# A hybrid decoder trunk on one core: the recurrence's decay by Exp, the heads' mean squares as columns, their root and split at other steps

## The chip, the cores and the metric

One core of a Trainium2 (trn2) chip runs the whole kernel. The metric is the time of one execution in microseconds; the median of the runs of the kernel before is compared with that of the kernel after. The engines are named as in the profile: PE (TensorE, matmuls; its weight loads are PEld), DVE (VectorE), ACT (ScalarE), POOL (GpSimd) and SP (SyncE, which issues the loads of the weights).

## The reference, cut to what matters

Two layers over 256 tokens of width 1024. Each layer is a token mixer, a channel mixer (a dense SwiGLU in layer 0, top 2 of 8 experts in layer 1) and a small gated embedding, each with norms around it. The change touches two places of the token mixer, the gated linear recurrence and the norm over each attention head:

```
r = sigmoid(blockdiag(u, w_a) + b_a);  i_gate = sigmoid(blockdiag(u, w_x) + b_x)
log_a = -8.0 * r * softplus(-lam)
a     = exp(log_a)
beta  = sqrt(-expm1(2.0 * log_a))
h[t]  = a[t] * h[t-1] + beta[t] * i_gate[t] * u[t]
...
o = (prob[:, 0] - lam * prob[:, 1]) @ v              # per head, 256 tokens x 128
o = o * rsqrt(mean(o * o, axis=-1) + 1e-6) * g_sub * (1.0 - lambda_init)
```

## The kernel before, in words

Every weight matrix comes in pieces ("chunks") of 128x2048 values of float32. A product of float32 accuracy is made of three products of a faster type: the chunk is split into a high part `whi` (ACT, line 630) and a low part `wlo` (DVE, line 1093), each in two halves of 1024 columns, and the activations into high and low parts in the same way (`HH`, `HL`; for the heads' outputs `YBH`, `YBL`, which lie in the same place). There are three slots for split chunks, so ACT splits chunk c+3 in step c, when PE has let go of each half of chunk c, and DVE follows it.

`mixer(layer)` is a list of steps c = 0 to 35, one chunk of weights each, written out by hand on every engine: each engine runs a loop over c and does, in the order of its code, what its `if` lines give to that step. The engines meet through semaphores alone. Each engine works strictly in order, so whatever stands behind a waiting instruction waits too.

- PE: in each step one chunk (48 products, `chunk8`, line 1743), then, by step: `gate_products` (2 to 5), `swap` for the rotary embedding (5 to 12), `scores` of head c-14 (line 1918, steps 14 to 21), `turn` (transposes of the weights of head c-16, line 1931, steps 16 to 23), `values` of head c-17, `head_square` of head c-18 (line 1951, steps 18 to 25). `inverse_row` (line 1866) transposes a column that is broadcast over 128 columns. Chunks 28 to 31 are the projection of the recurrence, 32 to 35 that of attention; chunk 32 is the first that needs `YBH` and `YBL`. Then `merge_out` (the output projection) and `embed` follow. In them `turn_x` (line 1854, four transposes of a half of X) waits for the sum of the residual. Later in layer 1, `logits` (line 2013) multiplies 128x128 weights by the 8 columns of the router.
- ACT: in each step first `hi` (the split, line 630, two halves), then copies of what PE made; `gate_functions` in steps 2 to 5 (sigmoids, and T2 = tanh(4 * r * softplus)), in step 6 the root of T2 (line 784), in step 7 T2 + 1 (786), in steps 12 and 16 the decay 2/(1 + T2) - 1 from the reciprocal (791); the exponentials of head c-14 (798, 803); Gelu in step 20 (775); Tanh of the merge gates in steps 21 to 28 (810); copies of the turned weights WT (817), of the head's output (824) and its square (825); the mean square of head c-18 copied (830); in step 28 the root of all reciprocal mean squares (836); in steps 29 and 30 the high part of the heads' outputs (840). After the mixer `square_z` (641) and `root_z` (664) make the norm of the merged output, and DVE adds it to X (line 1153).
- DVE: in each step first `lo` (line 1093), then by step: convolution (0 to 3), `rotate` (5 to 12), `recurrence_input` of tile c-8 (reciprocal line 1191, products 1192 and 1194, steps 8 to 15), `scan` in steps 13 and 17 (1200), gates scaled by the row norm (1158), `mask_max` of head c-14 (1224, 1227, 1230), `difference` of head c-15 (1235 to 1243), the reciprocal of a head's mean square in steps 19 to 26 (1334), `normalise_heads` in steps 28 and 29 (1250), `split_heads` in steps 30 and 31 (1256).
- POOL loads, once `split_heads` is through (`s_yb`), a row of gains for the norm behind the mixer. SP only issues the loads of the chunks.

The tanh form of the recurrence: with T2 = tanh(z), z = -log_a / 2, the decay is a = (1 - T2)/(1 + T2) = 2/(1 + T2) - 1 and beta = 2 sqrt(T2)/(1 + T2). The mean square of a head is a sum over the 128 partitions; a product with a matrix of ones (`ONES` as weights) gives it on every partition at once, as 128x256 values, equal in all rows.

## Time and profile before

| | before |
|---|---|
| median of 3 runs | 1862.76 us (1862.08 to 1863.0) |
| the profiled execution | 1862.89 us |
| its span, first to last instruction | 1861.2 us |
| mean granted clock of PE | 0.995 |
| PE busy | 1808.3 us, 97% of the span |
| DVE busy | 1541.8 us, 83% |
| ACT busy | 1307.3 us, 70% |
| POOL busy | 80.6 us, 4% |
| PE's share of the chain that ended last | 82% (DVE 11%, ACT 6%, issue 2%) |

The time is that of an execution, the span lies inside it: 1.7 us of the profiled execution lie around its span. Busy shares are means over stages with different limits; the two mixers (about 24 to 290 us and 570 to 835 us of the span) are where the change acts. A line of the timeline gives start, duration, engine, source line, operation, the tiles out<-in, and in brackets how long the engine had stood idle before it and what ended that; a line of the chain gives start, duration and what ran. "x4" at the end joins four instructions. Consecutive instructions of one engine overlap by about 0.1 us in the timeline, so starts are the better measure of a step.

### The profile page before, as it was taken

Reading aid. Unit: us, or ns where it says so; the run is one execution under the profiler, and the core shown is the slowest. Engines: PE = TensorE matmul, PEld = TensorE weight load, DVE = VectorE, ACT = ScalarE, POOL = GpSimd, SP = SyncE. Lnnn points to the kernel's source line nnn. Section 1 sums busy time; section 2 is a strip of 40 time slices with the busy share of each in tenths; the row PEclk is TensorE's granted clock in tenths of the full one; section 3 lists DMA queues with packets and bytes.
Section 4 is the critical chain, followed back from the end, with each engine's and each line's share of the span. In section 5 each row is a group of like instructions: output and inputs, shape, how many; then the busy total and the mean of one; then the engine's idle time right before and its main releaser. Section 6 shows DMA issues by size and latency. Waiting matters only on the chain.

```text
span 1861.2 us, 29663 instructions
## 1 busy us (share of the span) xinstructions
PE 1808.3 (97%) x10489; PEld 1573.7 (85%) x10489; DVE 1541.8 (83%) x1973; ACT 1307.3 (70%) x1730; POOL 80.6 (4%) x73
## 2 busy tenths in 40 slices
PE   6999999999999999999999999999999999999997
PEld 6998999999879988987888888888888888888785
DVE  7898877666468898768998989989899888998996
ACT  6656646444467557547878888788888887888776
POOL 1000000000010000002001000010000000000300
PEclk9999999999999999999999999999999999999999
DMA  9543456555554443557999999999999999999991
GB/s 304 161 159 130 165 172 201 183 181 198 197 173 144 160 159 114 182 194 222 390 381 385 378 372 386 368 380 380 372 387 365 382 386 366 385 372 378 391 365 54
DMA packets 274002, 512.82 MB, mean 276 GB/s; under 512 B 9731, under 2 KB 113029, under 8 KB 273925
## 3 DMA queue, kind: packets, MB, share of 16 engines
q1 hardware_dynamic: 268400, 493.81, 74.6%
q0 software_dynamic: 5200, 17.86, 2.8%
q8 instruction: 49, 0.80, 0.2%
q14 instruction: 29, 0.23, 0.0%
q10 hardware_dynamic: 324, 0.12, 0.0%
HBM read 503.87 MB, written 7.88 MB: 275 GB/s over the span
## 4 chain that ended last, share of the span: by engine, by line
PE 82%; DVE 11%; ACT 6%; issue 2%; DMA 0%; SPq 0%; DVEq 0%; ACTq 0%
PE bank L1743 77%; DVE wlo L1093 4%; ACT whi L630 2%; PE bank L2198 1%; DVE T L1191 1%; PE bank L1898 1%; ACT SC L803 1%; ACT SQJ L641 1%; DVE SC L1227 1%; DVE RIN L1200 0%; ACT HH L688 0%; PE bank L2208 0%; ACT SC L798 0%; PE bank L1854 0%; ACT L731 0%
## 5 line engine op out<-in xcount | busy, mean ns | idle before, releaser
L630 ACT ACTIVATE whi<-raw 128x1024 fp32r<-128x1024 f32 x880 | 920.4, 1059 | 330.7 <-PE bank L1743 322.4
L1093 DVE TENSOR_TENSOR wlo<-raw,whi 128x1024 fp32r<-128x1024 f32 x880 | 1030.2, 1222 | 127.1 <-ACT whi L630 123.7
L1743 PE MATMUL bank<-HH,whi 128*128 128x256 f32 x1296 | 372.6, 287 | 3.0 <-DVE HL L1256 3.0
L1743 PE MATMUL bank<-HL,whi 128*128 128x256 f32 x1296 | 362.4, 280 | 0.0
L1743 PE MATMUL bank<-HH,wlo 128*128 128x256 f32 x1296 | 362.3, 280 | 0.0
L1743 PE MATMUL bank<-whi,XGH 128*128 128x512 f32 x896 | 358.4, 400 | 1.4 <-DVE wlo L1093 1.0
L1743 PE MATMUL bank<-whi,XGL 128*128 128x512 f32 x896 | 352.2, 393 | 0.0
L1743 PE MATMUL bank<-wlo,XGH 128*128 128x512 f32 x896 | 348.9, 389 | 0.0
L1743 PEld LDWEIGHTS bank<-HH,whi 128*128 128x128 f32 x1296 | 244.1, 188 | 7.5 <-issue 6.9
L1743 PEld LDWEIGHTS bank<-HL,whi 128*128 128x128 f32 x1296 | 244.4, 189 | 3.5 <-issue 2.9
L1743 PEld LDWEIGHTS bank<-HH,wlo 128*128 128x128 f32 x1296 | 246.3, 190 | 0.0
L1743 PEld LDWEIGHTS bank<-whi,XGL 128*128 128x128 f32 x896 | 168.6, 188 | 39.6
L1743 PEld LDWEIGHTS bank<-wlo,XGH 128*128 128x128 f32 x896 | 168.8, 188 | 35.5
L1743 PEld LDWEIGHTS bank<-whi,XGH 128*128 128x128 f32 x896 | 169.0, 189 | 35.1 <-DVE wlo L1093 2.3
L1743 PE MATMUL bank<-whi,ATH 128*128 128x512 f32 x448 | 178.6, 399 | 0.0
L1743 PE MATMUL bank<-whi,ATL 128*128 128x512 f32 x448 | 175.7, 392 | 0.0
L1743 PE MATMUL bank<-wlo,ATH 128*128 128x512 f32 x448 | 174.0, 388 | 0.0
L1743 PEld LDWEIGHTS bank<-whi,ATL 128*128 128x128 f32 x448 | 84.1, 188 | 19.7
L1743 PEld LDWEIGHTS bank<-wlo,ATH 128*128 128x128 f32 x448 | 84.2, 188 | 17.8
L1743 PEld LDWEIGHTS bank<-whi,ATH 128*128 128x128 f32 x448 | 84.3, 188 | 16.0
L1442 DVE TENSOR_TENSOR wlo<-raw,whi 128x1024 fp32r<-128x1024 f32 x56 | 68.3, 1224 | 35.4 <-ACT whi L905 32.9
L905 ACT ACTIVATE whi<-raw 128x1024 fp32r<-128x1024 f32 x56 | 58.9, 1057 | 47.7 <-PE bank L1743 47.7
(348 smaller groups left out, 2123.4 us busy)
## 6 DMA issues: line engine op xcount, KB each, us to landing
raw<-in_moe_w_gate_dram SPq DMA_DIRECT2D x112, 1024.0 KB, 7.3
raw<-in_moe_w_up_dram SPq DMA_DIRECT2D x112, 1024.0 KB, 7.9
raw<-in_moe_w_down_dram SPq DMA_DIRECT2D x112, 1024.0 KB, 6.5
raw<-in_w_in_dram SPq DMA_DIRECT2D x56, 1024.0 KB, 5.1
raw<-in_ffn_w_gate_dram SPq DMA_DIRECT2D x14, 1024.0 KB, 5.0
raw<-in_ffn_w_up_dram SPq DMA_DIRECT2D x14, 1024.0 KB, 5.0
raw<-in_ffn_w_down_dram SPq DMA_DIRECT2D x14, 1024.0 KB, 4.9
raw<-in_w_proj_a_dram SPq DMA_DIRECT2D x8, 1024.0 KB, 5.2
```

Of the source, the lines that this page charges most:

```text
L630: nc.scalar.activation(whi[b % SPL][:, r], raw[b % RAW][:, r], ACT.Copy).then_inc(s_hi, 1)
L641: nc.scalar.activation(SQJ[:, :], src, ACT.Square, accum_out=sums).then_inc(s, 1)
L803: ins = nc.scalar.activation(r, r, ACT.Exp, bias=AMX[:, q, 2 + m:3 + m], scale=HD ** -0.5, accum_out=ASUM[:, q, 2 + m:3 + m])
L905: nc.scalar.activation(whi[nb % SPL][:, r], raw[nb % RAW][:, r], ACT.Copy).then_inc(s_hi, 1)
L1093: v.tensor_tensor(wlo[b % SPL][:, r], raw[b % RAW][:, r], whi[b % SPL][:, r].bitcast(F32), ALU.subtract).then_inc(s_lo, 1)
L1191: link(v.reciprocal(T2[:, i, :], T2[:, i, :]))
L1227: ins = v.tensor_tensor_reduce(SC[:, q, SEQ * (m + 1):SEQ * (m + 2)], B[4 + m][:, P:P + SEQ], MASK[:, :], 1.0, -3e38, ALU.add, ALU.max, AM ...
L1442: v.tensor_tensor(wlo[nb % SPL][:, r], raw[nb % RAW][:, r], whi[nb % SPL][:, r].bitcast(F32), ALU.subtract).then_inc(s_lo, 1)
L1743: ins = mm(dst, a, b, start=start and n == 0, stop=stop and n == 2, skip_group_check=True)
L1898: ins = mm(bank[:, SEQ * kind:SEQ * kind + SEQ], BD[:, kind, t, :], U[:, t, :], start=True, stop=True)
L2198: ins = nc.tensor.transpose(B[6][:, P * i:P * i + P], MA[:, f % 2, P * i:P * i + P], IDENT[:, :])
```

## The change

**Recurrence.** Tanh now goes into a tile of its own, `TH` (the place of K, whose keys are not made yet), and T2 keeps the gate r. In steps 7 and 8 ACT makes the decay from it directly, T2 = Exp(-8 * softplus * r), four tiles of 128x256 in each (`decays`); the factor is a new column set `SPNEG`, one product more among the constants. Since 2/(1 + tanh z) = 1 + a, beta is sqrt(TH) * (1 + a), one instruction of DVE. The eight reciprocals of T2 on DVE, T2 + 1 on ACT and the two copies of steps 12 and 16 are gone, and DVE waits for the decays at tiles 0 and 4.

**Heads' mean squares.** `head_square` now takes the squares as weights, block by block of 128 tokens, and multiplies them by one column of ones: two columns of sums for each head, tokens on the partitions, 128x16 for all heads. One Sqrt of ACT in step 25 and one reciprocal of DVE in step 25 cover all heads. In step 26 PE spreads them over the partitions again with 16 transposes of broadcast columns into banks 4 to 7 (`head_rows`). DVE multiplies the heads' outputs by these banks in steps 26 and 27 (four instructions of 128x512 in place of two of 128x1024), ACT and DVE split them in steps 27, 28 and 28, 29. The eight copies of ACT (line 830), the eight reciprocals of DVE (line 1334) and the two roots of ACT (line 836) are gone.

```diff
@@ -145,7 +145,9 @@
         SINR = at("SINR", o_sga + 7 * KB, [P, SEQ])
         top = o_sga + 8 * KB
         assert top <= end, (top, end)
-        OALL, MSALL = Q, K
+        OALL, TH = Q, K
+        SPNEG = SM[:, 72:88]
+        HSD, HRS = SM[:, 0:16], SM[:, 16:32]
         YBH, YBL = HH, HL
 
         FH = at("FH", a0 + 16 * KB, [P, FT, SEQ], F32R)
@@ -264,7 +266,6 @@
         s_ga = sem("s_ga")
         s_sq = sem("s_sq")
         s_iu = sem("s_iu")
-        s_den = sem("s_den")
         s_bl = sem("s_bl")
         s_al = sem("s_al")
         s_rt = sem("s_rt")
@@ -287,7 +288,7 @@
         s_oc = sem("s_oc")
         s_om = sem("s_om")
         s_or = sem("s_or")
-        s_oe = sem("s_oe")
+        s_hr = sem("s_hr")
         s_os = sem("s_os")
         s_yf = sem("s_yf")
         s_ybh = sem("s_ybh")
@@ -746,8 +747,15 @@
                     nc.scalar.activation(IG[:, t, :], bank[:, SEQ:], ACT.Sigmoid, bias=V2[:, 96 + col:97 + col])
                     if layer == 0 and t == 0:
                         act.wait_ge(s_c2, 1)
-                    ins = nc.scalar.activation(T2[:, t, :], T2[:, t, :], ACT.Tanh, scale=SPLAM[:, col:col + 1])
-                    ins.then_inc(s_ga, 1)
+                    nc.scalar.activation(TH[:, t, :], T2[:, t, :], ACT.Tanh,
+                                         scale=SPLAM[:, col:col + 1]).then_inc(s_ga, 1)
+
+            def decays(layer, g):
+
+                for t in range(4 * g, 4 * g + 4):
+                    col = layer * KT + t
+                    ins = nc.scalar.activation(T2[:, t, :], T2[:, t, :], ACT.Exp, scale=SPNEG[:, col:col + 1])
+                ins.then_inc(s_al, 1)
 
             def mixer(layer):
                 b = BASE[layer]
@@ -781,14 +789,9 @@
                     if c == 6:
                         act.wait_ge(s_ga, KT * (layer + 1))
                         act.wait_ge(s_iu, layer + 1)
-                        nc.scalar.activation(SQ[:, :, :], T2[:, :, :], ACT.Sqrt).then_inc(s_sq, 1)
-                    if c == 7:
-                        nc.scalar.activation(T2[:, :, :], T2[:, :, :], ACT.Copy, bias=1.0).then_inc(s_den, 1)
-                    if c in (12, 16):
-                        g = (c - 12) // 4
-                        act.wait_ge(s_bl, KT * layer + 4 * g + 4)
-                        r = T2[:, 4 * g:4 * g + 4, :]
-                        nc.scalar.activation(r, r, ACT.Copy, bias=-1.0, scale=2.0).then_inc(s_al, 1)
+                        nc.scalar.activation(SQ[:, :, :], TH[:, :, :], ACT.Sqrt).then_inc(s_sq, 1)
+                    if c in (7, 8):
+                        decays(layer, c - 7)
                     h = c - 14
                     if 0 <= h < HEADS:
                         n = HEADS * layer + h
@@ -823,19 +826,12 @@
                             act.wait_ge(s_om, n - 1)
                         nc.scalar.activation(OALL[:, h, :], B[7][:, 0:SEQ], ACT.Copy)
                         nc.scalar.activation(OSQ[:, h % 2, :], B[7][:, 0:SEQ], ACT.Square).then_inc(s_oc, 1)
-                    h = c - 18
-                    if 0 <= h < HEADS:
-                        n = HEADS * layer + h
-                        act.wait_ge(s_om, n + 1)
-                        nc.scalar.activation(MSALL[:, h, :], B[3][:, 0:SEQ], ACT.Copy, bias=EPS,
-                                             scale=1.0 / P).then_inc(s_oe, 1)
-                    if c == 28:
-                        act.wait_ge(s_or, HEADS * (layer + 1))
-                        for g in range(2):
-                            r = MSALL[:, 4 * g:4 * g + 4, :]
-                            nc.scalar.activation(r, r, ACT.Sqrt).then_inc(s_os, 1)
-                    if c in (29, 30):
-                        g = c - 29
+                    if c == 25:
+                        act.wait_ge(s_om, HEADS * (layer + 1))
+                        nc.scalar.activation(HSD[:, :], B[3][:, 0:2 * HEADS], ACT.Sqrt, bias=EPSC[:, 0:1],
+                                             scale=1.0 / P).then_inc(s_os, 1)
+                    if c in (27, 28):
+                        g = c - 27
                         act.wait_ge(s_yf, 2 * layer + g + 1)
                         nc.scalar.activation(YBH[:, 4 * g:4 * g + 4, :], OALL[:, 4 * g:4 * g + 4, :],
                                              ACT.Copy).then_inc(s_ybh, 1)
@@ -1185,12 +1181,12 @@
             def recurrence_input(layer, i):
 
                 if i == 0:
-                    dve.wait_ge(s_den, layer + 1)
                     dve.wait_ge(s_sq, layer + 1)
                     dve.wait_ge(s_iu, layer + 1)
-                link(v.reciprocal(T2[:, i, :], T2[:, i, :]))
-                link(v.scalar_tensor_tensor(out=SQ[:, i, :], in0=SQ[:, i, :], scalar=2.0, in1=T2[:, i, :],
-                                            op0=ALU.mult, op1=ALU.mult))
+                if i % 4 == 0:
+                    dve.wait_ge(s_al, 2 * layer + i // 4 + 1)
+                link(v.scalar_tensor_tensor(out=SQ[:, i, :], in0=T2[:, i, :], scalar=1.0, in1=SQ[:, i, :],
+                                            op0=ALU.add, op1=ALU.mult))
                 v.tensor_tensor(IG[:, i, :], IG[:, i, :], SQ[:, i, :], ALU.mult).then_inc(s_bl, 1)
 
             def scan(layer, g):
@@ -1245,10 +1241,12 @@
                                        op1=ALU.add).then_inc(s_df, 1)
 
             def normalise_heads(layer, g):
-                ms, o = (t[:, 4 * g:4 * g + 4, :] for t in (MSALL, OALL))
-                dve.wait_ge(s_os, 2 * layer + g + 1)
-                v.scalar_tensor_tensor(out=o, in0=o, scalar=GSUB[:, layer:layer + 1], in1=ms, op0=ALU.mult,
-                                       op1=ALU.mult).then_inc(s_yf, 1)
+                dve.wait_ge(s_hr, 2 * layer + g + 1)
+                for i in (4 * g, 4 * g + 2):
+                    o = OALL[:, i:i + 2, :]
+                    ins = v.scalar_tensor_tensor(out=o, in0=o, scalar=GSUB[:, layer:layer + 1], in1=bank2(4 + i // 2),
+                                                 op0=ALU.mult, op1=ALU.mult)
+                ins.then_inc(s_yf, 1)
 
             def split_heads(layer, g):
                 dve.wait_ge(s_ybh, 2 * layer + g + 1)
@@ -1273,6 +1271,7 @@
                     link(v.scalar_tensor_tensor(out=poly, in0=poly, scalar=1.0 / n, in1=s2, op0=ALU.add, op1=ALU.mult))
                 link(v.scalar_tensor_tensor(out=poly, in0=poly, scalar=1.0, in1=s1, op0=ALU.add, op1=ALU.mult))
                 link(v.scalar_tensor_tensor(out=poly, in0=poly, scalar=2.0, in1=SM[:, 32:48], op0=ALU.mult, op1=ALU.add))
+                v.tensor_scalar(SPNEG, poly, -8.0, None, ALU.mult)
                 v.tensor_scalar(SPLAM[:, :], poly, 4.0, None, ALU.mult).then_inc(s_c2, 1)
 
             def mixer(layer):
@@ -1328,14 +1327,13 @@
                             dve.wait_ge(s_tg, 8 * layer + 8)
                         v.scalar_tensor_tensor(out=pair(SGA, i), in0=pair(SGA, i), scalar=1.0, in1=bank2(c % 3),
                                                op0=ALU.add, op1=ALU.mult).then_inc(s_evd, 1)
-                    if 19 <= c < 27:
-                        h = c - 19
-                        dve.wait_ge(s_oe, HEADS * layer + h + 1)
-                        v.reciprocal(MSALL[:, h, :], MSALL[:, h, :]).then_inc(s_or, 1)
+                    if c == 25:
+                        dve.wait_ge(s_os, layer + 1)
+                        v.reciprocal(HRS[:, :], HSD[:, :]).then_inc(s_or, 1)
+                    if c in (26, 27):
+                        normalise_heads(layer, c - 26)
                     if c in (28, 29):
-                        normalise_heads(layer, c - 28)
-                    if c in (30, 31):
-                        split_heads(layer, c - 30)
+                        split_heads(layer, c - 28)
                     if 32 <= c < 36:
                         i = c - 32
                         if c == 35:
@@ -1946,9 +1944,17 @@
             def head_square(layer, h):
                 n = HEADS * layer + h
                 pe.wait_ge(s_oc, n + 1)
-                if h:
-                    pe.wait_ge(s_oe, n)
-                mm(B[3][:, 0:SEQ], ONES[:, :], OSQ[:, h % 2, :], start=True, stop=True).then_inc(s_om, 1)
+                for b in range(BLK):
+                    ins = mm(B[3][:, 2 * h + b:2 * h + b + 1], OSQ[:, h % 2, P * b:P * b + P], ONES[:, 0:1],
+                             start=True, stop=True, skip_group_check=True)
+                ins.then_inc(s_om, 1)
+
+            def head_rows(layer, g):
+                pe.wait_ge(s_or, layer + 1)
+                for i in range(8 * g, 8 * g + 8):
+                    ins = nc.tensor.transpose(B[4 + i // 4][:, P * (i % 4):P * (i % 4) + P],
+                                              HRS[:, i:i + 1].to_broadcast([P, P]), IDENT[:, :])
+                ins.then_inc(s_hr, 1)
 
             def mixer(layer):
                 b = BASE[layer]
@@ -1990,6 +1996,9 @@
                         values(layer, c - 17)
                     if 18 <= c < 26:
                         head_square(layer, c - 18)
+                    if c == 26:
+                        head_rows(layer, 0)
+                        head_rows(layer, 1)
 
             def merge_out(layer):
 
```

## Rows read from the trace of the kernel before

**Rows 1.** Windows (steps 15 to 22, 23 to 32): us, busy of PE, PEld, DVE, ACT, POOL, clock, DMA
```profile
127.70:187.36 59.66, 54.54 (x439) 49.85 (x439) 51.49 (x138) 40.29 (x103) 0.00 (x0) 1.00 0.43 141
187.36:246.66 59.30, 57.77 (x483) 57.03 (x483) 48.56 (x49) 36.51 (x49) 0.00 (x0) 1.00 0.49 162
```

**Rows 2.** Waits, layer 0's mixer: who <- for whom, us in total, times, longest
```profile
PE bank L1931 <- ACT WT L817: 3.9, 3, 1.4
...
PE bank L1743 <- DVE HL L1256: 1.5, 1, 1.5
```

**Rows 3.** Timeline of PE: scores of step 15, transposes of step 22
```profile
127.68 0.49 PE L1918 MATMUL bank<-K,Q 64*128 64x128 f32 x4 [0.85 <-DVE AMX L1230]
...
187.36 0.52 PE L1931 MATMUL bank<-IDENT,SC 128*128 128x128 f32 x3 [1.34 <-ACT WT L817]
```

**Rows 4.** Timeline of DVE: splits of steps 14 to 18 and 21, first maximum of step 14
```profile
123.95 2.36 DVE L1093 TENSOR_TENSOR wlo<-raw,whi 128x1024 fp32r<-128x1024 f32 x2
126.23 0.29 DVE L1224 CUSTOM_DVE_ANT_0 SC<-bank,MASK 128x128 f32<-128x128 f32 x1
...
130.51 2.36 DVE L1093 TENSOR_TENSOR wlo<-raw,whi 128x1024 fp32r<-128x1024 f32 x2 [0.31 <-ACT whi L630]
...
138.26 2.35 DVE L1093 TENSOR_TENSOR wlo<-raw,whi 128x1024 fp32r<-128x1024 f32 x2
...
145.77 2.36 DVE L1093 TENSOR_TENSOR wlo<-raw,whi 128x1024 fp32r<-128x1024 f32 x2 [1.68 <-ACT whi L630]
...
154.00 2.36 DVE L1093 TENSOR_TENSOR wlo<-raw,whi 128x1024 fp32r<-128x1024 f32 x2
...
180.15 2.36 DVE L1093 TENSOR_TENSOR wlo<-raw,whi 128x1024 fp32r<-128x1024 f32 x2 [1.97 <-ACT whi L630]
```

**Rows 5.** Timeline of ACT: step 14 and the start of 15; step 20
```profile
120.16 1.06 ACT L630 ACTIVATE whi<-raw 128x1024 fp32r<-128x1024 f32 x1 [1.70 <-PE bank L1743]
...
127.66 0.40 ACT L798 ACTIVATE SC<-SC,AMX 128x128 f32<-128x128 f32 x1 [4.42 <-DVE AMX L1230]
...
129.43 1.04 ACT L630 ACTIVATE whi<-raw 128x1024 fp32r<-128x1024 f32 x1
...
169.58 2.01 ACT L630 ACTIVATE whi<-raw 128x1024 fp32r<-128x1024 f32 x2
171.60 1.28 ACT L775 ACT_TABLE_LOAD   x1
172.90 1.92 ACT L775 ACTIVATE GEL<-GEL 128x2048 f32<-128x2048 f32 x1
```

**Rows 6.** Single lines of the source, whole span: duration in ns, min/median/max
```profile
L1191 DVE RECIPROCAL T<-T x16: 1743/1746/1749, 86.9 to 680.9; 128x256 f32<-128x256 f32 x16
L1866 PE MATMUL bank<-IDENT,STAT x6: 270/270/271, 30.4 to 576.0; 128*128 128x128 f32 x6
```

**Rows 7.** The chain of waits: start us, us, what
```profile
161.09 0.28 ACT K L830
...
189.22 5.66 PE bank L1743 x48
...
208.49 0.43 PE bank L1951 x2
...
286.29 0.44 PE bank L1854 x4
...
837.88 1.69 PE bank L2013 x16
```

**Rows 8.** Timelines of ACT and DVE behind layer 0's mixer: the root, the residual's sum
```profile
284.31 0.29 ACT L664 ACTIVATE STAT<-STAT 128x1 f32<-128x1 f32 x1
...
285.05 1.41 DVE L1153 SCALAR_TENSOR_TENSOR X<-ZG,STAT,X 128x512 f32<-128x512 f32 x2
```

**Rows 9.** Windows in layer 1: step 17, and the router's products
```profile
688.00:692.00 4.00, 2.57 (x16) 2.01 (x16) 2.29 (x6) 3.94 (x11) 0.00 (x0) 0.79 0.60 209
...
831.00:848.00 17.00, 15.85 (x95) 13.52 (x93) 11.45 (x35) 14.45 (x38) 4.58 (x8) 1.00 0.64 168
```

## The prediction, made before the result was known

> **What bounds the kernel now.** I read the windows first, then the waits, then the timelines of PE, VectorE (DVE) and ScalarE (ACT) side by side. Both mixers run the same list of steps, so I work out layer 0 and count it twice. In steps 23 to 32 PE is busy 57.77 of 59.30 us, with 10.7 us idle on DVE and 22.8 on ACT; in steps 15 to 22 PE is busy 54.54 of 59.66 us [rows 1], and 0.85 us more it stood at the edge of that window [rows 3]: 6.0 us. The list of waits puts 3.9 of them down to ACT's copy of WT, and beside them names 1.5 us for the low half of the head outputs, at step 32 [rows 2]. 6.0 and 1.5 us a mixer are what PE can win, small gaps inside a step aside.
>
> Where the 6.0 us come from takes two engines. PE is through chunk 14 at 120.16, when it lets go of the buffer that ACT waits for [rows 5]; DVE masks that step's scores only at 126.23, and neither this row nor the one at 123.95 prints a wait [rows 4]: DVE itself is 6 us late. Each of its steps from 8 on holds a reciprocal of T2 of 1.75 us [rows 6]. From there a loop closes: DVE splits (lo) and takes the maxima, ACT exponentiates, copies what PE made and splits the next chunk (hi), and only then DVE can split. DVE's splits of steps 15 to 18 start at 130.51, 138.26, 145.77 and 154.00, that of step 21 at 180.15 [rows 4]: turns of 7.75, 7.51, 8.23 and three together 26.15 us. At 138.26 no wait is printed: DVE was late, its reciprocal counts. At 145.77 and 180.15 it waits 1.7 and 2.0 us for ACT: a shorter DVE gains nothing there, only a shorter ACT. At 154.00 DVE is late by its scan, which stays.
>
> **The change part by part.** *Reciprocals of T2 out, Exp in.* DVE loses 16 reciprocals of 1.75 us over both mixers [rows 6]. In steps 8 to 13 PE never waits, so those six of a mixer's eight pay only through the lag they leave. Without them DVE keeps pace, and step 14 starts from ACT's second split at 120.16. A half split of ACT leads to DVE's by 1.08 us (129.43 to 130.51), DVE's half takes 1.14 (half of 123.95 to 126.23), and from the maxima to ACT's exponentials it is 1.43 (126.23 to 127.66) [rows 4, 5]: they start at 123.81 instead of 127.66. From there to DVE's next split is 2.85 us as before (127.66 to 130.51): 126.66 instead of 130.51, **3.85 us earlier**. In the next turn ACT's second split waits for PE's chunk, done at 126.83 (127.68 less the wait of 0.85 [rows 3]); 1.08 + 1.14 + 1.43 + 2.85 = 6.50 later, at 133.33, comes the next split. This turn takes 6.67 instead of 7.75, **1.08 us less**. The turn of 7.51 is ACT's and stays; that of 8.23 stays for the scan.
>
> The new work on ACT is eight Exp of 128x256 a mixer in steps 7 and 8. Two of 128x128 and two of 128x256 took 1.77 us (127.66 to 129.43 [rows 5]), so four of 128x256 take 1.8 to 3.5; a 2048-wide copy in step 7 and two 1024-wide ones in steps 12 and 16 go. The load of Exp's table moves from before step 14's exponential to step 7. PE runs on chunks split three steps ahead and never waits there, so this costs nothing; if that cover were gone, up to 3 us. DVE's new waits for the decays, at steps 8 and 12, stand ahead of its first use, lo and the next rotation queue behind them, and PE's swap behind these; the Exp ended a step before: nothing. The one product more (128x16, once) delays ACT's first Tanh by less than a reciprocal's 1.75 us, behind PE's products: nothing.
>
> *Mean squares as columns.* ACT's copy of each head's mean square, 0.28 us, is in the loop in steps 18 to 20 [rows 7]: three turns, **0.8 us**. The eight reciprocals of K lie beside ACT's part of the loop or where DVE is idle: nothing. PE's two records of 256 columns took 0.43 us a head; now each of two blocks has 128x128 weights and one column. The nearest row is the router's product with 8 columns, 16 records in 1.69 us [rows 7]: four records a head are 0.42 us, **no difference**. Bounds: 0.2 us less a head (two records) to 0.7 more (four times the 0.27 of a lone record [rows 6]).
>
> *Sixteen transposes at step 26* are new, and PE is the bound there: four take 0.44 us on the path [rows 7], so **1.8 us are lost**. The other end is 0.27 us each, the duration of one transpose of a broadcast column [rows 6]: 4.3 us. I take the pipelined value, since four such take less than two durations. Their input is early: after chunk 25 come half a split (1.08), a Tanh no longer than a half split, a load (1.28) and two tiny operations of 0.3, some 4.1 us at most, while PE needs 5.66 for chunk 26.
>
> *Root and split earlier.* DVE normalises at steps 26 and 27, ACT splits at 27 and 28, DVE at 28 and 29; PE reads at 32, so the stall of **1.5 us** goes. Next late would be the weight split for chunk 32, done in step 29, in time. DVE's waits at 25 and 26 (under 1 us each; lo is ahead of them in its queue, the next lo behind) fall where it is idle 10.7 us: nothing. POOL's load of the gain row waits for the split and is issued earlier.
>
> *Table loads.* Sqrt at step 25 stands between the Tanh of 25 and 26, and the norm's root comes after the mixer: loads at 25, 26 and the root instead of one at 28. Each takes 1.28 us, the next activation starts 20 ns behind [rows 5]. Those of 25 and 26 fall where ACT has 2 us idle a step. The third does not: the root ran at 284.31 without a wait, DVE's add began at 285.05 and had its first half at 285.76 (half of 1.41), PE's transpose of it began at 286.29 [rows 7, 8]. 0.5 us of slack against 1.3: **0.8 us lost**; bounds 0 and 2.1.
>
> The Trainium skill ("ScalarE: Activation LUTs", What ACT_TABLE_LOAD costs) speaks against this part: it puts a switch of tables at about 1283 ns for the load and 1380 ns of drain, 2.66 us, by which the sum would be 1.4 us a mixer worse. The trace agrees on the load and shows no drain around it [rows 5].
>
> **Sum.** 3.85 + 1.08 + 0.8 + 1.5 - 1.8 - 0.8 = 4.6 us a mixer, 9.2 us for two. From the profiled execution's 1862.89 us: 1853.7. It stands 0.1 us over the median of the runs, so I give **1853.6 us**. About 0.2%, 3.7 us, is what a measurement of this kernel can tell from no change.
>
> **Rivals.** *(1) The lag was not the reciprocals'.* If something else holds step 14's maxima back, the first 3.85 us stay: 0.8 us a mixer left, 1861.2 us, no measurable change. For it: most turns are ACT's. Against: DVE prints no wait at 123.95 and 126.23. Chance 0.10.
> *(2) Transposes in single file.* 4.3 us instead of 1.8: 2.5 us a mixer more, 1858.6. Against it the 0.44 us for four. 0.10.
> *(3) A switch of tables holds ACT for twice the load's 1.28 us.* Then 2.1 us instead of 0.8 are lost at the root, 1856.2. Against it the 20 ns behind the load. 0.07. This is the page's figure as a mechanism.
> *(4) PE's waits go altogether and the load at the root is covered.* 6.0 + 1.5 - 1.8 = 5.7 us a mixer, 1851.4. 0.09.
> *(5) Slower: the clock falls behind step 26.* In layer 1 the granted clock was 0.79 of full in 688 to 692 us, where PE was busy 2.57 of 4.00 us [rows 9]. If transposes and one-column products made it fall to the lower of its levels (1.2 GHz), each chunk of 5.66 us takes 11.3. The gain of 4.6 us a mixer is gone after 4.6 us' worth of products at that level, and from 6.5 us' worth on the kernel is measurably slower; two chunks cost 11.3 us a mixer, 1876. Against it: the 32 router products and 16 transposes in 831 to 848 us, all at 1.00 [rows 9]. 0.04.
>
> **How the numbers follow.** The forecast has 0.60, its own range being 1851 to 1857 (table load 0 to 2.1, turns 0.3 us each). Faster by over 0.2% is below 1859.0: 0.60 + 0.10 + 0.07 + 0.09 = 0.86. Within: rival 1, 0.10. Slower: rival 5, 0.04. The range 1850.5 to 1859.0 takes in rivals 2 to 4 and leaves out 0.14 and a little.
>
> **What would show it.** Right: step 14's scores are masked at about 122.4 us; DVE's turns read 6.7, 7.5, 8.2 and 25.3 for three; PE's transposes of step 22 start at 181.6 instead of 187.36; no wait of PE at step 32; sixteen transposes in 1.8 us; a load ahead of the root and behind it a wait of PE for X of 0.8 us; DVE busy 56 us less. Wrong: PE waiting for the maxima at step 15 as before or for the 16 reciprocals at step 26, a clock under 0.95 in steps 26 to 30, or waits of PE for weights in steps 8 to 13 because Exp came in the way of hi.

## The result and the profile after

The changed kernel takes 1847.2 us (median of 5 executions, 1845.92 to 1853.16) against 1862.81 of the kernel before (5 executions): ratio 0.9925, 95% interval 0.9914 to 0.9935. Faster, as forecast, but by 15.6 us and not by 9.2, and below the range. The five times lie in two groups: 1845.92, 1846.68 and 1847.2, and then 1852.61 and 1853.16. The profiled execution took 1845.92 us, of which 1844.3 are its span. From its page, the span and the busy time of each engine:

```profile
span 1844.3 us, 29748 instructions
PE 1801.3 (98%) x10553; PEld 1568.6 (85%) x10553; DVE 1490.6 (81%) x1948; ACT 1302.6 (71%) x1726; POOL 80.7 (4%) x73
```

DVE is busy 51.2 us less (forecast 56), 1541.8 to 1490.6. The windows of layer 0's mixer, steps 15 to 22 and then 23 to 32 [rows 1]:

```profile
126.55:181.60 55.05, 53.21 (x448) 49.43 (x447) 44.15 (x132) 35.85 (x90) 0.00 (x0) 1.00 0.41 135
181.60:240.40 58.80, 58.79 (x503) 58.43 (x504) 39.12 (x44) 33.98 (x43) 0.58 (x1) 1.00 0.50 170
```

In the first stretch PE stands still for 1.84 us where it stood for 5.12. In the second it stands for none, sixteen transposes included, and the clock is 1.00. DVE's splits of steps 14 to 18, with the first maximum of step 14 [rows 4]:

```profile
119.78 2.47 DVE L1089 TENSOR_TENSOR wlo<-raw,whi 128x1024 fp32r<-128x1024 f32 x2
122.16 0.28 DVE L1220 CUSTOM_DVE_ANT_0 SC<-bank,MASK 128x128 f32<-128x128 f32 x1
...
126.44 2.51 DVE L1089 TENSOR_TENSOR wlo<-raw,whi 128x1024 fp32r<-128x1024 f32 x2 [2.10 <-ACT whi L631]
...
133.15 2.52 DVE L1089 TENSOR_TENSOR wlo<-raw,whi 128x1024 fp32r<-128x1024 f32 x2 [0.50 <-ACT whi L631]
...
140.83 2.36 DVE L1089 TENSOR_TENSOR wlo<-raw,whi 128x1024 fp32r<-128x1024 f32 x2 [1.68 <-ACT whi L631]
...
149.06 2.36 DVE L1089 TENSOR_TENSOR wlo<-raw,whi 128x1024 fp32r<-128x1024 f32 x2
```

DVE now waits for ACT in every turn but that of the scan: the lag is gone, and the turns are 6.71, 7.68 and 8.23 us. PE's timeline: the scores of step 15 and the transposes of step 22 [rows 3], one group of head squares, the sixteen transposes, and the first transposes of X behind the mixer:

```profile
126.53 0.49 PE L1916 MATMUL bank<-K,Q 64*128 64x128 f32 x4
...
181.60 0.52 PE L1929 MATMUL bank<-IDENT,SC 128*128 128x128 f32 x3 [1.26 <-ACT WT L820]
...
202.20 0.50 PE L1948 MATMUL bank<-ONES,OSQ 128*128 128x1 f32 x4
...
208.30 1.91 PE L1955 MATMUL bank<-IDENT,SM 128*128 128x128 f32 x16
...
279.24 0.40 PE L1741 MATMUL bank<-whi,YAL 128*128 128x512 f32 x1
280.27 0.66 PE L1852 MATMUL bank<-IDENT,X 128*128 128x128 f32 x4 [0.63 <-DVE X L1149]
```

ACT's timeline behind the mixer has the table load ahead of the root [rows 8]:

```profile
277.64 1.28 ACT L665 ACT_TABLE_LOAD   x1
278.94 0.29 ACT L665 ACTIVATE STAT<-STAT 128x1 f32<-128x1 f32 x1
```

**Where the rest came from.** From the scores of step 14 to the transposes of step 22, the profiled executions differ by 5.53 us in layer 0 (67.31 to 61.78); up to the transposes of X behind mixer 0, by 5.9 (286.13 to 280.27). Mixer 1 gives 5.05 (254.95 to 249.90, from the transposes ahead of it to those of X). Before, the granted clock dips between the layers (0.54 in 557 to 559 us); in the change's profile it stays at 1.00 there, which takes 1.3 us out. Behind mixer 1 it dips in both, at another moment of the work, which adds 1.2. The 5.6 us that are left came between the two mixers, in the dense layer, which the change does not touch. That stretch begins with two transposes of a broadcast column inside its second chunk and reaches the down projection's first product, which reads FH, after some 1,300 products of 128x256. The kernel before:

```profile
304.45 0.38 PE L1866 MATMUL bank<-IDENT,STAT 128*128 128x128 f32 x2
...
454.49 0.40 PE L1743 MATMUL bank<-whi,FH 128*128 128x512 f32 x1
```

and the kernel after:

```profile
298.63 0.38 PE L1864 MATMUL bank<-IDENT,STAT 128*128 128x128 f32 x2
...
443.04 0.39 PE L1741 MATMUL bank<-whi,FH 128*128 128x512 f32 x1
```

150.04 us became 144.41, with the same instructions. Two windows of 20 us inside the stretch (us, PE busy, clock, DMA share, GB/s), before:

```profile
320.00:340.00 20.00, 20.00 (x172) 1.00 0.60 195
400.00:420.00 20.00, 20.00 (x173) 1.00 0.54 173
```

and after:

```profile
320.00:340.00 20.00, 20.00 (x179) 1.00 0.56 186
400.00:420.00 20.00, 20.00 (x179) 1.00 0.54 178
```

PE is busy all the time in both, at full clock in both, with a like share of DMA (0.54 to 0.60), and 172 or 173 products fall into 20 us in the one and 179 in the other, those that reach over an edge counted in. By the starts of single products, one comes every 117.8 ns or every 113.3. I call them the slow and the quick pace.

Both paces also occur inside the mixers of every profile, and at one place there they go with a stall of PE. Before, PE stands still inside chunk 32 and runs what follows of chunks 32 to 35 at the slow pace; after, there is no stall and the pace is quick. The stall, and a window of 10 us behind it, before:

```profile
246.66 0.36 PE L1743 MATMUL bank<-HH,whi 128*128 128x256 f32 x1 [1.51 <-DVE HL L1256]
...
250.00:260.00 10.00, 10.00 (x87) 1.00 0.48 156
```

and such a window after:

```profile
245.00:255.00 10.00, 10.00 (x90) 1.00 0.57 181
```

From the first to the last of their 192 products, chunks 32 to 35 took 24.14 us before, in both mixers, and 21.65 after, in both: 2.49 us less. Of these the stall is 1.67 by the starts of the products (1.51 are printed as a wait). The experiments ask two things: does each part of the change pay what the sum said, and is the quick pace the change's work?

### The profile page after: what moved, and what is told of

It reads as the page before. It is cut to its first block, busy times and chain, and to the rows that moved or that the text cites. A ratio compares the mean times of both kernels' runs of the same rounds, so it can differ in the third digit from the quotient of the medians.

```text
span 1844.3 us, 29748 instructions
## 1 busy us (share of the span) xinstructions
PE 1801.3 (98%) x10553; PEld 1568.6 (85%) x10553; DVE 1490.6 (81%) x1948; ACT 1302.6 (71%) x1726; POOL 80.7 (4%) x73
## 4 chain that ended last, share of the span: by engine, by line
PE 87%; DVE 6%; ACT 5%; issue 1%; DMA 0%; DVEq 0%; SPq 0%; ACTq 0%
PE bank L1741 81%; DVE wlo L1089 2%; PE bank L2207 1%; ACT whi L631 1%; PE bank L1905 1%; PE bank L1896 1%; ACT SQJ L642 1%; ACT SC L806 1%; DVE X L1149 0%; DVE HL L1107 0%; PE bank L2217 0%; PE bank L1852 0%; DVE SC L1223 0%; ACT L732 0%; DMA IFR<-in_inv_freq_dram 0%
## 5 line engine op out<-in xcount | busy, mean ns | idle before, releaser
L1741 PE MATMUL bank<-HH,whi 128*128 128x256 f32 x1296 | 367.6, 284 | 0.0
```

The costliest lines, as they stand in the source:

```text
L1741: ins = mm(dst, a, b, start=start and n == 0, stop=stop and n == 2, skip_group_check=True)
```

## The experiments

All times are medians in us; where two kernels are compared, their runs are on one chip unless the text says otherwise.

**1. The change again, and each of its parts alone.** The changed kernel; Exp in the recurrence alone; the heads' part alone (each is the diff's one half); and the change with the table of Sqrt loaded at step 29:

```diff
+                    if c == 29:
+                        table(ACT.Sqrt)
```

> The changed kernel as it is, once more. Its times so far fall in two groups, 1845.9 to 1847.2 us (three) and 1852.6 and 1853.2 us (two), where the kernel before gave 1862.1 to 1864.0 five times. Theory A (pace): outside the mixers the products of 128x256 run in one of two paces, one every 113.3 ns or one every 117.8 ns, and each holds for long; the profiled run of after has the quick one through the whole dense stretch (300 to 440 us and on), before the slow one. Then these times fall in the two groups again, 6 us apart, and the profile's pace in the dense stretch tells its group: 1852 to 1853.5 us with 117.8 ns, 1846 to 1847.5 us with 113.3 ns. Rival B: the 6 us beyond my sum belong to the change itself (less traffic of DVE and ACT); then the dense stretch has 113.3 ns in every profile of this kernel, and two groups need another cause.

> Only the recurrence's part: Tanh into a tile of its own, decays by Exp in steps 7 and 8, no reciprocals of T2; the heads stay as before. By my sum it is worth 3.85 + 1.08 us a mixer: 9.9 us under before, about 1853 us at the slow pace of the dense stretch, about 1847 at the quick one. The split of step 21 on DVE starts 4.9 us earlier than before (about 175.2 us), PE's stall of 1.5 us at step 32 stays. Rival: if the loop between DVE and ACT were bound by the copies and reciprocals of the mean squares too, less than 3 us a mixer would come.

> Only the heads' part: mean squares as columns, one root and one reciprocal in step 25, sixteen transposes in step 26, normalisation and split earlier; the recurrence stays as before with its reciprocals. By my sum 0.8 + 1.5 - 1.8 - 0.8 = -0.3 us a mixer (a loss of 0.3), with what the profile of after shows (0.09 us less per head's square, 0.63 us at the table load) a gain of 0.3 us: 1862 to 1863 us at the slow pace of the dense stretch, about 1856.5 at the quick one. Rival: if the copies and reciprocals of the mean squares were what binds steps 18 to 21, 2 us a mixer or more.

> The changed kernel with one tiny Sqrt more on ACT in step 29 of each mixer, behind the last Tanh, so that the table is in before the norm's root. Mechanism expected: the load in front of the root (277.64 us in the profile of after) goes, and with it PE's wait of 0.63 us for X in front of its first transposes: 1.3 us less than the changed kernel over both mixers at equal pace, so 1844.5 to 1846 or 1851 to 1852 us. If the load were hidden there anyway, no difference but the wait's other cause would show.

Measured, against 1862.58 for the kernel before: the change 1850.86 (ratio 0.9944, interval 0.9931 to 0.9957), Exp alone 1850.88 (0.9940, 0.9927 to 0.9953), heads alone 1859.1 (0.9975, 0.9964 to 0.9987), early load 1849.71 (0.9940, 0.9928 to 0.9953). The profiles agree with the sum far better than the medians. Exp alone takes 62.59 us from scores 14 to transposes 22, and its stall at step 32 stays:

```profile
242.17 0.36 PE L1746 MATMUL bank<-HH,whi 128*128 128x256 f32 x1 [1.51 <-DVE HL L1258]
```

Heads alone takes 66.49 (0.8 less than before's 67.31, the forecast's K copies), without a stall. The profile of the early load shows the load at 228.32, behind a half split of ACT for which it had waited 1.43 us, and no wait of PE for X: the transposes of X start 0.23 us behind the product ahead of them, as in the kernel before, where the change has 1.03 (279.24 to 280.27).

The medians do not add up, and the pace is why. The dense stretch takes 144.40 us in the repeated change's profile (an execution of 1847.17; its other four took 1850.29 to 1853.5). It takes 150.04, 150.03 and 150.04 in those of Exp alone, heads alone and the early load. Heads alone, run 12 times, has six times from 1854.17 to 1857.43 and six from 1860.76 to 1863.74. The pairs of pace and time that were expected did not all come: Exp alone took 1851.78 at the slow pace, where 1853 was expected, and the early load 1848.68, where it was 1851 to 1852. A time alone does not tell the pace, for the dips of the clock move it too.

**2. Can the pace be set?** One idle product of 512 columns behind the two transposes, which nothing reads, in four kernels: the change, the kernel before, the change with early load, and Exp alone.

```diff
+            def lock():
+                mm(B[7][:, :], SWAP[:, :], X[:, 0, 0:512], start=True, stop=True)
...
-                        chunk8(b + n, (HH, HL), 1, lambda k: inverse_row(1, 6) if k == 4 else None)
+                        chunk8(b + n, (HH, HL), 1, lambda k: (inverse_row(1, 6), lock()) if k == 4 else None)
```

> The changed kernel with one idle float32 product of 128x512 (0.43 us, result unused) put on PE right behind the two transposes in the dense stretch's second chunk. In the six profiles so far every chunk behind such a product (the rotary swap of steps 5 to 12) ran at 113.3 ns a product, while those transposes left 117.8 in four and 113.3 in two, for the whole dense stretch. Theory A (the pace of PE's products is set by what stands in front and then holds): quick pace in the dense stretch in the profile, the time between the stretch's transposes and those of the next mixer about 265 instead of 271 us, and all times in the lower group, about 1846 to 1848 us, none at 1850 to 1853. Theory B (pace is chance, whatever stands in front): the times spread as before, 1846 to 1853. Theory C (the pace is set by DVE's and ACT's traffic): no change either.

> The kernel before, with the same idle product at the same place and nothing else. Theory A: its dense stretch, slow so far, goes to 113.3 ns a product: 28 chunks of 48 products, 4.5 ns each, 6 us less, and 0.4 us for the product: about 1857 us. Theories B and C, or the rival that the 6 us belong to the change of the mixers: 1862 to 1864 us, 117.8 ns in the profile.

> The changed kernel with both the early table load (step 29) and the idle product. Theory A and the load's exposure of 0.6 us a mixer add up: 1.3 us under the changed kernel with the idle product alone, 1844.5 to 1846.5 us, the lowest of all so far. Without theory A: 1848.5 to 1852.5 as with the early load alone.

> The recurrence's part alone with the idle product. At equal pace of the dense stretch this part is worth 11 to 12 us by its runs (1850.9 against 1862.6 us); theory A gives 5.5 us less than without the idle product: 1845 to 1846 us. Then the heads' part is worth about nothing at equal pace (the changed kernel with the idle product less this one: within 1.5 us). Without theory A 1850 to 1852 us.

All four profiles have the quick pace in the dense stretch. The kernel before with the idle product:

```profile
303.06 0.38 PE L1869 MATMUL bank<-IDENT,STAT 128*128 128x128 f32 x2
303.28 1.02 PE L1864 MATMUL bank<-X,SWAP 128*128 128x512 f32 x2
...
448.32 0.39 PE L1743 MATMUL bank<-whi,FH 128*128 128x512 f32 x1
```

145.26 us, the idle work's 0.86 included; the other three take 145.25 to 145.27. The medians are 1858.12 for before (eleven executions, 1856.14 to 1859.43), 1848.28 for the change (1846.3 to 1849.35), 1845.79 with early load (1845.49 to 1846.07) and 1846.54 for Exp alone (1846.04 to 1849.2). The kernel before without the product took 1861.66 on that chip. So work added to the path of a kernel whose PE is 97% busy made it 3.5 us faster (ratio 0.9979, interval 0.9970 to 0.9988).

At this common pace the change can be read: 1858.12 to 1848.28 is **-9.8 us**, where the sum said -9.2. Its parts are smaller than the 3 us over which the times of one kernel spread, so for them the profiles count, from the scores of step 14 to the transposes of X in both mixers. Exp's part takes 4.5 and 4.1 us out there (the sum's first two terms: 4.9 each); the medians say -11.6. With the heads' part on top the two stretches together are 0.4 us shorter (the sum's other four terms: 0.6 longer); the medians say +1.7, with times in the same band (1846.3 to 1849.35 against 1846.04 to 1849.2), so that it is worth nothing that these runs can tell. The early load takes 0.8 us out of each mixer, 1.6 in all, where 1.3 was expected; the medians say 2.5, but between the two profiled executions another 1.4 us lie behind layer 1's mixer, in the routing, where the clocks dip at different moments, and are not the load's.

**3. Must it be a product?** In place of it four idle transposes, in the kernel before:

```diff
+            def lock():
+                for i in range(4):
+                    nc.tensor.transpose(B[7][:, P * i:P * i + P], X[:, 0, P * i:P * i + P], IDENT[:, :])
```

> A control for the pace: the kernel before with four idle transposes of 128x128 (0.44 us, as long as the idle product) at the product's place. Theory A in the narrow form (a float32 product of 512 columns leaves the quick pace, transposes leave the slow one): 117.8 ns a product behind it, 150.0 us from the stretch's own transposes to the first product of the down projection, plus 0.4; time 1862 to 1864 us. In the wide form (any 0.4 us between transposes and products resets the pace): 145.3 us and 1858 us, as with the product.

```profile
304.50 0.38 PE L1870 MATMUL bank<-IDENT,STAT 128*128 128x128 f32 x2
304.71 0.60 PE L1865 MATMUL bank<-IDENT,X 128*128 128x128 f32 x4
...
449.33 0.39 PE L1743 MATMUL bank<-whi,FH 128*128 128x512 f32 x1
```

144.83 us: the quick pace, and 1856.85 against 1862.7 (0.9969, interval 0.9957 to 0.9980). It need not be a product: other work of PE behind the two transposes is enough, and it may be half as long, for the transposes add 0.43 us to the stretch and the product 0.86 (the expectation took them as equally long).

**4. The reciprocals' cost by itself.** Exp alone with the idle product, and on top an idle reciprocal per tile (no one reads its result), for tiles 0 to 5 (steps 8 to 13) in one kernel and 6 and 7 (steps 14 and 15) in the other:

```diff
+                if i < 6:
+                    link(v.reciprocal(SQJ[:, 0:SEQ], RINV[:, :]))
```

> The recurrence's part with the idle product, and an idle reciprocal of 128x256 on DVE (1.75 us, result unused) back in steps 8 to 13, six a mixer. My first term says that these six cost by the lag alone that they leave in step 14: 3.7 us a mixer, 7.4 us in all, 1853.5 to 1855 us; DVE masks step 14's scores at about 126 us instead of 122.6. Rival (the lag was not theirs): under 2 us.

> The same with the idle reciprocals in steps 14 and 15 alone, two a mixer. My second term says that only step 15's counts, as it makes DVE later than ACT in one turn of the loop: 1.1 to 1.4 us a mixer, 2.2 to 2.8 us in all, 1849 us. Rival (ACT's part of the loop hides it too): nothing.

With the first six 1855.27, 8.7 us above the 1846.54 without (which was timed on another chip); from scores 14 to transposes 22 it is 66.09 us for 62.61, +3.5 a mixer, and the maxima of step 14 start at 125.60 instead of 122.29 (expected: about 126). With the last two 1850.16, 3.6 above (expected: 2.2 to 2.8), and 63.61 us, +1.0 a mixer; the turn from step 15 to 16 is 7.91 us for 6.71. Both terms of the sum, 3.85 and 1.08, are so found again from the other side. Together they bring 4.5 us a mixer back, of the 4.7 that Exp's part takes out of this stretch (67.31 to 62.61).

**5. A version that beats both.** Exp alone with the idle product still waits 1.51 us at step 32. Its split of the heads moved one step forward:

```diff
-                    if c in (30, 31):
-                        split_heads(layer, c - 30)
+                    if c in (29, 30):
+                        split_heads(layer, c - 29)
```

> A version that may beat all: the recurrence's part with the idle product, the heads as before but DVE's split of their outputs one step earlier (steps 29 and 30 instead of 30 and 31). My reading of the 1.5 us that PE waits at step 32 is that the second split alone is late; the high part it needs is ready in step 30. Then the wait goes without columns, transposes or further table loads: 1.5 us a mixer less than the recurrence's part with the idle product, 1843 to 1844 us. Rival: DVE waits for ACT in step 29 or 30 and its weight splits come late, no gain.

1842.88 us (1842.33 to 1843.08; 0.9894, interval 0.9878 to 0.9911), and PE waits no more at step 32. That is 3.7 us less than without this edit (the two were timed on different chips), where two stalls of 1.5 make 3.0, and the fastest kernel of the study. The profiles show the rest: chunks 32 to 35 take 21.65 us for 24.14 in both mixers, as in the change, and 0.36 us of it is given back in the output projection. The heads' part bought the same with sixteen transposes and a table load; this edit of one step needs neither.

Over all 18 profiles this place tells more of the pace than the dense stretch. In the 22 mixers without the stall, chunks 32 to 35 run at the quick pace in every one. In the 14 with it, what follows the stall is slow in 11 (24.14 us) and quick in 3 (23.43). So here the quick pace comes with an edit that takes the stall out, whichever of the two does it, and it is worth 0.7 us a mixer beyond the stall; the three exceptions say that a stall makes the slow pace likely and not certain.

**6. Is the pace drawn anew at each execution?** The changed kernel three times and heads alone once more, untouched, one execution each.

> The changed kernel unchanged, one look. If pace is drawn anew in each execution behind the two transposes, the profile's own time goes with the pace: 144.4 us from those transposes to the first down product and a time of 1845.5 to 1848 us, or 150.0 us and 1850 to 1853.5 us. If the change itself made the pace quick, 144.4 us every time.

> The same kernel and the same expectation as the look before it: the pair (144.4 us, 1845.5 to 1848 us) or the pair (150.0 us, 1850 to 1853.5 us), and if it is chance, not the same pair in all looks at this kernel.

> Once more the same kernel and the same expectation: one of the two pairs; a third value of the stretch would speak against two paces.

> The heads' part alone once more, whose twelve times fell in two groups, 1854.2 to 1857.4 and 1860.8 to 1863.7 us, its profile being of the upper one with 150.0 us in the stretch. Either 150.0 us again and 1861 to 1864 us, or 144.4 us and 1854 to 1857.5 us.

The change took 1851.26, 1851.25 and 1850.96 us, heads alone 1861.16. The first of them:

```profile
298.52 0.38 PE L1864 MATMUL bank<-IDENT,STAT 128*128 128x128 f32 x2
...
448.56 0.40 PE L1741 MATMUL bank<-whi,FH 128*128 128x512 f32 x1
```

and a window in that stretch:

```profile
320.00:340.00 20.00, 20.00 (x172) 1.00 0.50 166
```

150.04 us, and 150.03, 150.04 and 150.03 in the other three. One and the same program has either pace, and the two it was given in its profiles, at 1845.92 and 1847.17 us, against the three from 1850.96 up, lie on the mean 4.6 us apart, where the paces alone make 5.6 and the clock's dips differ. Of the changed kernel's 13 executions four took under 1847.3 and nine over 1850.2, so that its usual time is the upper one: the median of all 13 is 1850.96 us.

## Why the prediction was right and where it failed

**The lag: right.** Step 14's scores are masked at 122.16 (forecast 122.4, before 126.23), and the splits stand at 126.44, 133.15, 140.83 and 149.06 (forecast 126.66, 133.33, 140.84). The split of step 21 starts at 174.39, by the forecast's turns 174.4; the transposes of step 22 at 181.60, forecast 181.6. The way to get there, adding up the loop's parts from ACT's second split, held to 0.25 us. Experiment 4 shows that it was the reciprocals: put back, they bring 3.5 and 1.0 us.

**Step 32: the stall right, its price too small.** The stall is gone, for which the sum has 1.5 us a mixer. Chunks 32 to 35 became 2.49 us shorter, since the slow pace behind the stall went with it. In mixer 1 the output projection gives 0.36 us back (19.12 to 19.48 us), in mixer 0 it does not: 2.5 and 2.1 us where 1.5 was forecast.

**The K copies: right.** The 0.8 us are found in experiment 1.

**The sixteen transposes: right.** They start 0.109 us apart, 1.75 us for all, forecast 1.8; the stretch from the last head square to chunk 32 grew by 1.95 us (33.71 to 35.66).

**Head squares: right.** The chain of waits puts 0.34 us down to a head's four records, where it had 0.43 for two, but 0.1 more to the chunk behind them (5.76 us). By the starts of the products around them a head takes the same as before, within 0.02 us, and the four start 0.112 us apart, as the router's do. No difference was forecast.

**The load at the root: right.** The transposes of X start 1.03 us behind the product ahead of them instead of 0.23: 0.80 us, forecast 0.8, of which the profile prints 0.63 as a wait. No drain stands in the timeline around it: the root starts 20 ns behind the load. The Trainium skill's figure for a whole switch (2.66 us, "ScalarE: Activation LUTs", What ACT_TABLE_LOAD costs) would have made 2.1 us, an estimate with the forecast's 0.5 us of slack; the trace does not bear it out.

**The step that failed: the sum.** It adds up the two mixers and takes the 1.3 ms outside them as fixed, and a chunk of 48 products as 5.66 us wherever it stands. A chunk takes 5.66 us at the slow pace and 5.45 at the quick one. In the profile before, the dense stretch had the slow pace; in the profiled execution behind the changed kernel's first median, 1845.92 us, it had the quick one, a missing term of -5.6 us. The two other times of that lower group, the median 1847.2 among them, were not profiled, and their pace is inferred from their times. The range was built from the bounds of the change's own costs and had no room for it.

Which of the two times the measurement gave was luck: the repeat's median is 1850.86 and the three single executions took 1850.96 to 1851.26, all inside the range. At that pace the number fits the sum no better than to 2 us, though, for the two mixers gave more than the sum. In an execution of the change at the slow pace, 1851.26 us, the profile shows -5.98 us up to the end of mixer 0, -5.05 in mixer 1 and -0.6 in all the rest: 11.0 us from the mixers where the sum had 9.2. Over both, -11.1 come from steps 14 to 22 (forecast -11.5), -4.6 from chunks 32 to 35 and the output projection (forecast -3.0: the second term that was mis-sized, again by the pace), +3.9 between the last head square and chunk 32 (forecast +3.6), +1.6 ahead of X (forecast +1.6) and -0.75 ahead of step 14, where nothing was forecast and the runs show no cause. With the idle product in both kernels it is 9.8.

**Rivals.** (1), a lag that stays, fell by the row at 122.16 and by experiment 4. (2), 4.3 us of transposes, fell by their 1.75. (3), twice the load, fell by the 0.80 us ahead of X. (4) named 1851.4 us, close to the times at the slow pace, for a reason that did not happen: PE still waits 1.84 us in steps 15 to 22, and for X behind the load. (5) fell: clock 1.00 from 181.60 to 240.40. None of them was about work that the change leaves alone, nor about the pace.

**Open.** What chooses the pace was not found. In the dense stretch it is not the granted clock, the number of instructions or PE's waits, which are the same in the windows above, and the DMA share does not sort them (in those two windows 0.48 to 0.60 at the slow pace, 0.54 to 0.64 at the quick one, over all profiles). In the changed kernel's quick profile the first products behind the transposes are still slow and the quick ones begin at 299.44, 0.8 us behind the first transpose. In all ten profiles with a quick stretch the turn comes within six products, in eight of them one product behind an interval of 0.122 or 0.123 us; the eight slow ones have no such interval there and stay slow. What makes that interval is open. That the change makes the quick pace likelier (two profiles of five, and four times of 13 in the quick group, while the kernel before has only two of its 49 times under 1858.2, and its one profile is slow) is suggested and not shown. Nor is it shown why the idle work settles it.

## What to carry to other kernels

Where an engine prints no wait and is late all the same, follow its lag back to where it began, and add up the loop's parts: that gave each start to a quarter of a microsecond. Then compare the stretches that the change does not touch, before a difference of the whole is put down to it; counts of instructions in equal windows at equal clock show a change of pace in one row. A stall can cost more than its length, by the pace at which the engine goes on. And before heavy machinery is built to get rid of a stall, try to issue the late work one step earlier.

## What the runs showed of the hardware

- PE runs the same products of 128x256 at one of two paces, 113.3 or 117.8 ns each, at a granted clock of 1.00, and keeps one for a whole stretch: 144.4 or 150.0 us here. One program shows both in different executions.
- Behind a stall of 1.5 us inside chunk 32 the next 167 products ran at the slow pace in 11 of 14 mixers; without the stall they ran at the quick one in 22 of 22 (24.14 against 21.65 us for the four chunks).
- One idle product of 512 columns (0.86 us) or four idle transposes (0.4 us) behind two transposes gave the quick pace in all eight profiles of kernels that had them (145.25 to 145.27 us, and 144.83); of the ten without, two were quick.
- Products with 128x128 weights and one column start 0.112 us apart, the router's with eight columns the same; transposes of 128x128 start 0.109 us apart.
- A table load costs ACT its 1.28 us and 20 ns, in the three places where it can be seen here (171.60 before, 277.64 after, 228.32 in the early load).
